# An encoder layer in split float32 on one core: merge, up and output projections rearranged, attention records stored by SyncE's queue

## What is computed

```
h = rmsnorm(x) ; z = h @ w_in
a = pool_mixer(z[:, :512]) @ w_up_pool            # 4 window sizes, 128 channels each
o_g, lse_g = dilated window attention, 3 groups of 4 heads (width 64)
b = (sum_g softmax_g(lse)_g * o_g) @ w_up_attn    # "merge": 256 channels
gates = sigmoid(h @ w_gate + b_gate)              # 2 x 1024 channels, g_a and g_b
x = x + (g_a*a + g_b*b) @ w_out
x = x + (silu(h2 @ w_ffn_gate) * (h2 @ w_ffn_up)) @ w_ffn_down,  h2 = rmsnorm(x)
y = rmsnorm(x)
```

## Time and profile before

| what | value |
|---|---|
| three runs | 2791.15, 2797.35, 2797.04 us; median 2797.04 us |
| profiled execution | 2793.5 us, span 2791.7 us |
| mean granted TensorE clock | 0.971 of 2.4 GHz |
| busy: PE, PEld, DVE, ACT, POOL (us) | 2618.3, 2126.5, 1241.7, 1082.5, 1848.3 |
| transfers | 350.25 MB, 331.01 MB of it in SP's queue, 17.09 MB in ACT's |

### The profile page before, as it was taken

How to read it: one execution, slowest core, us unless ns; L and a number is a source line. 1 busy time by engine, 2 the same in 40 slices (tenths; PEclk the granted TensorE clock), 3 DMA queues, 4 the chain that set the end, 5 groups by cost and what they waited for, 6 DMA issues and landing times.

```text
span 2791.7 us, 33643 instructions
## 1 busy us (share of the span) xinstructions
PE 2618.3 (94%) x12048; PEld 2126.5 (76%) x12048; DVE 1241.7 (44%) x1781; ACT 1082.5 (39%) x2108; POOL 1848.3 (66%) x1354
## 2 busy tenths in 40 slices
PE   5999999889799999899969999998897999998998
PEld 5887777668688888788758877776686888887886
DVE  5743556652322222344667435566433222223446
ACT  4224554333433333244542345543334233332444
POOL 6775445414688888798767654453257888886986
PEclk9999999999899999999979999999899999999999
DMA  3443445453133333363443434453522333334534
GB/s 122 121 144 99 134 140 144 136 197 101 58 101 102 99 106 114 108 201 114 150 149 110 149 99 138 140 157 134 196 83 68 111 95 103 107 93 143 192 117 140
DMA packets 334532, 350.25 MB, mean 125 GB/s; under 512 B 16800, under 2 KB 247584, under 8 KB 332576
## 3 DMA queue, kind: packets, MB, share of 16 engines
q1 hardware_dynamic: 317088, 331.01, 37.7%
q10 hardware_dynamic: 17280, 17.09, 1.8%
HBM read 248.75 MB, written 99.29 MB: 125 GB/s over the span
## 4 chain that ended last, share of the span: by engine, by line
PE 85%; DVE 5%; DMA 3%; POOL 2%; ACT 2%; issue 2%; SPq 1%; DVEq 0%; ACTq 0%
PE ps L829 27%; PE ps L831 26%; PE ps L830 26%; PE ps L894 2%; PE ps L864 2%; PE ps L849 1%; PE ps L876 1%; DMA gl<-sp_rows 1%; DMA xb<-x 1%; DVE xb L1427 1%; DMA wu_raw<-w_up_attn 1%; DVE pw L1550 1%; SPq L478 1%; DVE rec L1604 1%; DVE Y L1647 1%
## 5 line engine op out<-in xcount | busy, mean ns | idle before, releaser
L829 PE MATMUL ps<-S,t_hi 128*128 128x512 f32 x2296 | 928.5, 404 | 19.3 <-DVE v L1486 10.6
L831 PE MATMUL ps<-S,t_lo 128*128 128x512 f32 x2296 | 898.3, 391 | 0.0
L830 PE MATMUL ps<-S,t_hi 128*128 128x512 f32 x2296 | 897.4, 391 | 0.0
L829 PEld LDWEIGHTS ps<-S,t_hi 128*128 128x128 f32 x2296 | 433.2, 189 | 126.6 <-issue 38.4
L831 PEld LDWEIGHTS ps<-S,t_lo 128*128 128x128 f32 x2296 | 432.6, 188 | 92.3
L830 PEld LDWEIGHTS ps<-S,t_hi 128*128 128x128 f32 x2296 | 433.8, 189 | 78.7
L673 POOL TENSOR_TENSOR t_lo<-wraw,t_hi 128x512 fp32r<-128x512 f32 x190 | 249.0, 1311 | 265.0 <-ACT t_hi L1124 262.4
L673 POOL TENSOR_TENSOR t_lo<-wraw_ff,t_hi 128x512 fp32r<-128x512 f32 x220 | 282.8, 1286 | 77.0 <-ACT t_hi L1124 72.7
L1124 ACT CAST t_hi<-wraw_ff 128x512 fp32r<-128x512 f32 x220 | 137.0, 624 | 375.0 <-PE ps L831 372.3
L673 POOL TENSOR_TENSOR t_lo<-R,t_hi 128x512 fp32r<-128x512 f32 x154 | 232.1, 1511 | 64.5 <-ACT t_hi L1124 64.5
L1674 DVE TENSOR_TENSOR d_lo<-d_raw,d_hi 128x512 fp32r<-128x512 f32 x154 | 166.7, 1085 | 213.5 <-ACT d_hi L1294 213.5
(11 more groups left out here) (152 smaller groups left out, 4228.7 us busy)
## 6 DMA issues: line engine op xcount, KB each, us to landing
d_raw<-d_rows SPq DMA_DIRECT2D x154, 256.0 KB, 3.2
d_rows<-act_f SPq DMA_DIRECT2D x110, 256.0 KB, 2.1
wraw<-w_in SPq DMA_DIRECT2D x44, 512.0 KB, 6.1
wraw_ff<-w_ffn_gate SPq DMA_DIRECT2D x44, 512.0 KB, 4.8
wraw_ff<-w_ffn_up SPq DMA_DIRECT2D x44, 512.0 KB, 4.7
R<-w_ffn_down SPq DMA_DIRECT2D x88, 256.0 KB, 3.1
sp_rows<-gst SPq DMA_DIRECT2D x80, 256.0 KB, 2.5
wo_raw<-w_out SPq DMA_DIRECT2D x36, 512.0 KB, 3.2
```

Of the source, the lines that this page charges most:

```text
L829: nc.tensor.matmul(o_ps, w[0], r[0], start=begins, stop=False, skip_group_check=True)
L830: nc.tensor.matmul(o_ps, w[0], r[1], start=False, stop=False, skip_group_check=True)
L831: return nc.tensor.matmul(o_ps, w[1], r[0], start=False, stop=ends, skip_group_check=True)
```

## The change

**Records.** ACT only copies the unit's result; SP issues the store, in its list for product m the store of unit m - 67 (the unit is copied beside product m - 1). `load_records` stays at its place.

**Merge.** A batch takes six products in place of four; DVE does four of the six scalings, one per product, ACT the other two, as 16 activations of 64 columns each. The sums of batch 0 come at product 123, of batch 1 at 129. Transposes come after products 127 and 131. The mixer's rows 0 to 2 are loaded when batch 0 is merged, row 3 when both are, and each is split on its own.

**Up.** The first two steps' weights are loaded at product 120. The order of half steps on PE begins a0, a1, b0, b1, then as before. The first product waits for each k tile alone. SP loads up weights one step earlier in its list. On ACT a step is: `up_hi(j+2)`, the first sigmoid of j+1, `y_high(j)`, the second sigmoid of j+1. `out_hi(0)` follows at step 5, `out_hi(1)` at step 6.

**Out.** x is loaded in four parts between the tiles of `w_out`, after the last up product. Low parts 16 and 17 go from POOL to DVE, `mix_last` for pair 1 goes ahead of low part 15. The last three visits of round 3 are done for tile 6 and then for tile 7, and tile 6 is added and normed by itself.

**FFN.** The first four activation tiles of the down products are split within the last pair on ACT and DVE; the stores of the last activations move one down product later on SP.

```diff
-MT_AFTER = {MERGE0 + 9: 0, MERGE0 + 10: 1}
+MT_AFTER = {MERGE0 + 9: 0, MERGE0 + 13: 1}
+UP_ORDER = [(0, 0), (1, 0), (0, 1), (1, 1)] + [(j, a) for j in range(2, TT) for a in range(2)]
...
+N2_LAST = {(t, 21 + v): [15 + 3 * n + v] for n, t in enumerate(OUT_ROUNDS[-1][0]) for v in range(3)}
...
-        wu_at = [(XR + 20480, XR + 23552, XR + 26624), (WR + 16384, WR + 19456, WR + 22528)]
+        wu_at = [(XR + 25600, XR + 28672, XR + 20480), (WX + 12288, WX + 16640, XR + 16384)]
...
+            def store_record(s, unit):
...
+                sp.wait_ge(o_ready, due("o_ready", s, unit + 1))
...
+                sp.dma_start(by_res[qb // n, (qb % n) * P:(qb % n + 1) * P, :], o_st[:, unit % 4, :]
+                             ).then_inc(o_stored[unit % 4], 16)
...
+                    if 0 <= m - ATT0 - 2 < N_UNITS:
+                        store_record(s, m - ATT0 - 2)
...
-                    if m == MERGE0 + 9:
-                        sp.wait_ge(merged, due("merged", s, 2))
-                        for g in range(4):
-                            sp.dma_start(ml[g][:, :], mix_rows[g]).then_inc(ml_in[g], 16)
+                    if m == MERGE0 + 2:
                         load_up(s, 0)
+                        load_up(s, 1)
+                    if m == MERGE0 + 6:
+                        sp.wait_ge(mix_stored, due("mix_stored", s, 8))
+                        load_mixed(s, range(3), 1)
+                    if m == MERGE0 + 13:
+                        load_mixed(s, range(3, 4), 2)
...
-                sp.wait_ge(prod_done, due("prod_done", s, FRONT))
-                load_up(s, 1)
+                sp.wait_ge(t_ready, due("t_ready", s, FRONT))
+                load_gates(s, 1)
+                load_up(s, 2)
...
                 for j in range(2, TT):
-                    load_up(s, j)
+                    if j + 1 < TT:
+                        load_up(s, j + 1)
                     load_gates(s, j)
-                    if j == 5:
+                    if j == 4:
...
-                sp.wait_ge(up_full, due("up_full", s, 4 * (TT - 1)))
-                for t in range(TT):
-                    sp.dma_start(X[:, t, :], x_t[s, t]).then_inc(xr_in, 16)
-                for op in range(2, N_WO):
+                load_out(s, 2)
+                load_out(s, 3)
+                sp.wait_ge(up_full, due("up_full", s, 4 * TT))
+                for op in range(4, N_WO):
+                    if op < 8:
+                        for t in (2 * op - 8, 2 * op - 7):
+                            sp.dma_start(X[:, t, :], x_t[s, t]).then_inc(xr_in, 16)
                     load_out(s, op)
...
-                    if m == N_PROD + 2:
+                    if m == N_PROD + 3:
                         store_products(s, steps - 1)
...
                 mix_first(s, 1, 1)
                 out_low(s, 14)
+                mix_last(s, 1, 1)
                 out_low(s, 15)
-                mix_last(s, 1, 1)
-                out_low(s, 16)
-                out_low(s, 17)
...
+                for t in OUT_ROUNDS[-1][0]:
+                    for visit in range(len(VISITS) - 3, len(VISITS)):
+                        out_products(s, visit, (t,))
+                        part_transposes(s, 1, N2_LAST[t, visit])
...
+            def merge_scale(s, batch, pairs):
+
+                act.wait_ge(coef_ready, due("coef_ready", s, batch + 1))
+                r, g = rec[batch], GROUPS - 1
+                for q in pairs:
+                    for t in range(4):
+                        for h in range(2):
+                            o = r[:, t, 2 * g + q, h * HEAD:(h + 1) * HEAD]
+                            i = 4 * t + 2 * q + h
+                            ins = nc.scalar.activation(o, o, ACT.Copy, scale=d3[:, g, i:i + 1])
+                ins.then_inc(scaled, 1)
...
+                    if n == N_PAIRS - 1 and o > 2:
+                        part_hi(s, N_PROD + o - 3)
...
-                act.wait_ge(prod_done, due("prod_done", s, max(m - 3, N_PROD - 1)))
                 if d in (2, 3):
                     act.wait_ge(t_ready, due("t_ready", s, N_PROD))
+                elif d > 3:
+                    act.wait_ge(prod_done, due("prod_done", s, m - 3))
...
+                    if m in (MERGE0 + 2, MERGE0 + 3, MERGE0 + 8, MERGE0 + 9):
+                        merge_scale(s, (m - MERGE0) // 6, [(m - MERGE0) % 2])
+                    if m == MERGE0 + 4:
+                        up_hi(s, 0)
+                        up_hi(s, 1)
...
                 for j in range(TT):
-                    if j + 1 < TT:
-                        sigmoids(s, j + 1)
                     if j + 2 < TT:
                         up_hi(s, j + 2)
+                    if j + 1 < TT:
+                        sigmoid(s, j + 1, 0)
                     y_high(s, j)
-                    if j == TT - 2:
+                    if j + 1 < TT:
+                        sigmoid(s, j + 1, 1)
+                    if j in (TT - 3, TT - 2):
+                        out_hi(s, j - TT + 3)
```

More of the change, by code:

```diff
@@ L86, in pool_step @@
     return (e, stage) if 0 <= e < len(POOL_JOBS) else (None, None)
+UP_ORDER = [(0, 0), (1, 0), (0, 1), (1, 1)] + [(j, a) for j in range(2, TT) for a in range(2)]
+UP_COUNT = {(j, a, h): 2 * n + h + 1 for n, (j, a) in enumerate(UP_ORDER) for h in range(2)}
 OUT_ROUNDS = (((0, 1, 2), range(8)), ((3, 4, 5), range(7, -1, -1)), ((6, 7), range(8)))
@@ L254, in encoder @@
         both = [at(f"both{r}", WX + 4096 + 4096 * r, [4, 2, P]) for r in range(2)]
-        ml = [at(f"ml{g}", XR + 4096 * g, [T]) for g in range(4)]
+        ml = [at(f"ml{g}", XR + o, [T]) for g, o in enumerate((0, 4096, 8192, 12288))]
         mix_hi = [at(f"mix_hi{g}", SP_ * g, [T], F32R) for g in range(4)]
@@ L974, in pair_banks, with up_products, out_products @@
                     last[bank0(n) + b] = (reader[0], s, reader[1])
-            def up_products(s, j):
+            def up_products(s, j, a):
                 pe.wait_ge(wu_ready, due("wu_ready", s, j + 1))
                 r = j % 2
-                for c in range(4):
-                    h, b = c % 2, 4 * r + c
-                    first, rows = (0, list(zip(mix_hi, mix_lo))) if c < 2 else (4, list(zip(m_hi, m_lo)))
-                    if j == 0 and c == 0:
-                        pe.wait_ge(mixed_ready, due("mixed_ready", s, POOL_GROUPS))
-                    if j == 0 and c == 2:
-                        pe.wait_ge(mT_ready, due("mT_ready", s, 4))
+                first, rows = ((0, list(zip(mix_hi, mix_lo))), (4, list(zip(m_hi, m_lo))))[a]
+                for h in range(2):
+                    b = 4 * r + 2 * a + h
+                    if j == 0 and a == 1:
+                        pe.wait_ge(mT_ready, due("mT_ready", s, 2 * h + 2))
                     bank_read(b)
                     for k, hl in enumerate(rows):
+                        if j == 0 and a == 0 and h == 0:
+                            pe.wait_ge(mixed_ready, due("mixed_ready", s, k + 1))
                         w = [t[r][:, first + k, :] for t in (wu_hi, wu_lo)]
-                        ins = three(ps[:, b, :], w, [a[:, half(h)] for a in hl], k == 0, k == len(rows) - 1)
+                        ins = three(ps[:, b, :], w, [x[:, half(h)] for x in hl], k == 0, k == len(rows) - 1)
                     ins.then_inc(up_full, 1)
-                    last[b] = ("a_read" if c < 2 else "b_read", s, 2 * j + h + 1)
-            def out_products(s, visit):
+                    last[b] = (("a_read", "b_read")[a], s, 2 * j + h + 1)
+            def out_products(s, visit, tiles):
                 rnd, k, op = VISITS[visit]
-                tiles, v = OUT_ROUNDS[rnd][0], visit % 8
+                v = visit % 8
                 pe.wait_ge(wo_ready, due("wo_ready", s, op + 1))
@@ L1001, in out_products @@
                 r = SLOT_OF[op]
-                for idx, t in enumerate(tiles):
+                for t in tiles:
                     for n in range(2):
-                        b = 2 * idx + n
+                        b = 2 * OUT_ROUNDS[rnd][0].index(t) + n
                         if v == 0:
@@ L1392, in _ @@
                     ff_pair(s, n)
-                for m in range(N_PROD, N_PROD + 4):
-                    part_hi(s, m)
                 for m in range(N_PROD, N_OPS):
@@ L1648, in gated, with add_projected @@
                                  Y[:, :, 3:7:2, c].bitcast(F32), ALU.subtract).then_inc(y_ready, 1)
-            def add_projected(s, rnd):
-                for idx, t in enumerate(OUT_ROUNDS[rnd][0]):
+            def add_projected(s, *tiles):
+                for t in tiles:
                     for n in range(2):
@@ L1723, in _ @@
                         pooled_low(s, e)
[L1724 to L1739 removed]
+                    batch, step = divmod(m - MERGE0, 6)
+                    if batch in (0, 1):
+                        if step == 0:
+                            merge_differences(s, batch)
+                        elif step == 1:
+                            merge_coefficients(s, batch)
```

(16 more changed lines are left out.)

137 lines of the change are left out of this document (68 added, 69 removed).

## The result

The changed kernel takes **2715.96 us** (median of 4 runs, 2712.18 to 2717.12) against 2795.66 us for the kernel before on the same chip: ratio 0.9715, 95% interval 0.9698 to 0.9732. The forecast was 2712, its range 2686 to 2752. Where a difference is small I read the waits in the trace, not the time.

The account below looks back on a forecast made before the run. PE was taken to bound the kernel, busy 2618.3 of 2791.7 us. Gains of 26 + 30 + 18 + 9 = 83 us gave 2710.5 from the profiled execution or 2714 from the median; forecast 2712 us, range 2686 to 2752.

Parts of the forecast that it names:

- A, merge: Merge to first up product: waits for product 124's addition and the first up product go; gain 26 us, bounds 11 to 32.
- B, up: Up and first out round: gates' cycle shortens from 10.9 to 8.3 us a step; gain 30 us, bounds 14 to 39.
- The walk: Up steps followed at 8.3 us each from the first up product, giving new waits of 4.6 us a sequence.
- Rival 1: Up: the gates' cycle stays the bound at 9.1 us a step; 20 us less gain, 2732 us; chance 20%.
- C, last out round: Last out round: waits behind POOL's low parts and part of the last norm's go; gain 18 us, bounds 5 to 25.
- D, first down products: First down products: old waits go, about 4 us comes at the sixth; gain 9 us, bounds 5 to 14.
- Records: Record stores moved to SP's queue: landings of at most 6.9 us within 8.1 of cover; cost 0, up to 10.
- rival 5: Records in SP's queue land too late and slow the products with units; 2816 us at 10.3 us landing; chance 5%.
- rival 2: Merge keeps a wait, ACT standing in line for up weights and coefficients; 19 us less gain, about 2731; chance 13%.
- rival 3: All four stretches run dry of waits, upper bounds summing to 110 us; 2684 us; chance 7%.
- rival 4: Waits only change names, no part giving more than 2 us; 2790 us; chance 4%.
- Clock: PE time at the lower 1.2 GHz level, tied to waits, comes back: 2.6, 7, 3.5 and 1.5 us by window.

Follow-up runs that it names:

- edit 10: Changed kernel with the second batch's record loads three products later, behind the stores of two results: 2709.7 us, ratio 0.9699.
- edit 3: Changed kernel with both sigmoids of step j+1 ahead of the rounding of Y of step j on ACT: 2725.87 us, ratio 0.9752.
- the repeat: The changed kernel measured once more, with nothing altered: 2718.92 us, ratio 0.9730.
- edit 8: Changed kernel with all eight loads of x in one block ahead of the fifth `w_out` tile: 2731.39 us, ratio 0.9770.
- edit 6: Changed kernel with low parts 16 and 17 back on POOL, behind part 15: 2726.41 us, ratio 0.9754.
- edit 5: Changed kernel with the last three out visits done for tiles 6 and 7 together on PE: 2719.25 us, ratio 0.9726.
- edit 9: Changed kernel with the stores of the last activations' sums two down products later on SP: 2712.19 us, ratio 0.9708.
- Edit 1: Changed kernel with records stored from ACT's queue again, at once after the copy: 2717.95 us, ratio 0.9723.
- edit 2: Changed kernel with ACT's share of the merge scalings back on DVE, in the new order: 2719.16 us, ratio 0.9728.

## Why the prediction was right

**A, merge** (26; 25.2). The mechanism is right. The wait on product 124's addition is 0.2 us and the first up product waits for nothing. The late start stayed as said, with 1.75 and 0.54 us behind it, and edit 10 shows its cause. But the sum comes out so near by luck in part: 2.5 of the 25.2 us lie ahead of the merge, where the forecast had nothing. The merge gave 22.6: 1.83 and 1.85 us on ACT's copy of `u` in the second batch were not in the sum (ACT copies when DVE has written `gst`, which now stands between scalings), and its clock gave 3.4 us where 5.2 were booked. The fourth mixer row was ready in sequence 1 but 1.88 us late in sequence 2, which falls in B. That the early mixer rows and weights took out the 5.37 us before the first up product rests on the trace; no edit undoes them.

**B, up** (30; 27.2). The walk named waits of 0.6, then 1.0 and 1.0 to 2.6, and up to 1 for x; these add up to 2.6 to 5.2, and the 4.6 it used is not worked out further. The trace has 1.07, then 0.52 (on DVE's `gl`, which the walk did not have), 0.94 and 1.26: 3.8. The mechanism is right and the term that was mis-sized is the clock: 7 us were taken in each sequence, and it gave 6.6 in sequence 1 and 5.4 in sequence 2, where seven matmuls behind the 1.88 us wait for the mixer row run at the lower level. What the lower bound was built on was wrong too: a cycle of 9.1 us was to cost 16, and edit 3 shows a cycle of 9.3 that costs 7 (10 against the first median). Rival 1 would have been a smaller loss than its 2732. The price of moving x, "up to 1 us" at the later visits, held, but only for loads in turns with `w_out`: in one block they cost 12.5 us against the repeat (edit 8), so it is not the bytes but their order that decides.

**C, last out round** (18; 19.0). The list of what is left was 1.0 + 0.5 + 1.5 + 5.7; it is 0.97 + 0.76 + 1.01 + 6.22, besides 1.3 of small ones that were there before. Edit 6 puts the low parts on DVE at 7.5 us of it or more, so of C's parts this is the large one; `mix_last` took 2.3 us of waits in each sequence. The tile split was to take 1.5 us off the wait for the norm and to cost 1.5 for part 17; by edit 5 it takes 1.4 and costs 1.0.

**D, first down products** (9; 5.0, its lower bound). Both old waits went, and one of 3.58 and 3.40 us stands at the sixth product, where I took 4, for the reason given (edit 9). Missed were 1.07 us at the third, twice, for two sums of activations that POOL makes ahead of its low part. The clock was mis-sized as well: I booked a gain of 1 us, and D lost 0.7, since the down stage has 1.2 us more busy time than before (423.9 us before, 425.1 after, both sequences).

**Records** (0; 0). Edit 1. The reading behind it was wrong and did no harm: 6.9 us was taken for the longest landing of a record's store and is that of a load; the longest store took 6.0.

**The rivals.** Rival 1's pace did not come: a step takes 8.2 to 8.5 us and only the one with the two loads of `w_out` 9.05 and 9.75. Nor did rival 5's landings. Waits from the merge to the first up step did stay, as rival 2 had it, 7.85 us of them, but not by its mechanism: edit 10 leaves ACT's list as it is and they fall to 1.5, so it was DVE's late start that made them and not ACT standing in line for weights. Nor did all waits go (rival 3) or only change names (rival 4).

**Clock.** 5.2 + 14 + 7 + 1 = 27.2 us were booked; 4.9 + 11.9 + 7.3 - 0.7 = 23.5 came, to the rounding. In the second window of the earlier trace rows a clock of 0.94 went to 1.00 when the four waits of 2.4 to 4.2 us went. Behind the wait of 3.58 us that ended at 1152.30 the first matmul takes 0.59 us to the start of the next and the six after it 0.43 each, the lower level. But the length of a wait does not settle it: behind 1.07 us at 1140.25 the matmuls keep 0.23 us, and behind 3.40 us in sequence 2 no run of slower ones shows, while shortly behind 1.85 us at 1861.82 seven matmuls in a row take 0.43.

## What to carry to other kernels

Where one engine is busy for most of the span (94% here), list its waits with the step that is ahead of each in *another* engine's order, and move that step: nearly all of the 76 us came from order and from moving a few operations to another engine (edit 6), none from less work on PE. The clock that came back with the waits is 23.5 of them. In a queue that works in order, what stands ahead of a small transfer sets its time, so put bulk loads in groups with the small ones between (edits 8 and 10), and put stores that wait for something behind the loads that don't (edit 9). A producer's cycle that is slower than the engine it feeds seems to cost its lag over all steps less the lead it starts with (edit 3 alone speaks for it), so count both before pricing it.

## What the runs showed of the hardware that I had not expected

**Small DVE operations take on POOL's length.** POOL and DVE in the kernel after, between two products of the merge:

```profile
507.93 1.30 POOL L705 TENSOR_TENSOR t_lo<-wraw,t_hi 128x512 fp32r<-128x512 f32 x1 [0.90 <-ACT t_hi L1162]
...
507.95 1.30 DVE L1642 TENSOR_TENSOR den<-wden 128x16 f32<-128x16 f32 x1
509.29 0.17 DVE L1643 TENSOR_TENSOR den<-den,wden 128x16 f32<-128x16 f32 x1
```

Two operations on 16 columns, one after the other: the one that begins 0.02 us behind a POOL operation of 1.30 us takes 1.30, the next, in the gap before POOL's next at 509.31, takes 0.17. The trace here agrees with the Trainium skill (SBUF — State Buffer, Who interferes with whom), by which the engine that starts second waits for the other's whole operation. The loss here is set by the length of the other engine's instruction, so small operations lose most for their size.

**ACT's small scalings are no bargain by the element.** Eight of 64 columns take 2.02 us, 0.25 each; one scaling of DVE's covers the same 512 columns in 0.69 us (at 513.89 in the kernel after) to 1.81 (at 510.72). By edit 2 they bring nothing that the time shows.

**A store behind loads in one queue.** The store issued at 482.93, behind eight record loads, held its buffer until DVE went on at 490.53; with half the loads ahead of it (edit 10) it was issued at 480.01 and DVE did not wait. The store at 482.93, from issue to landing, in the kernel after:

```profile
DMA to landing us min/median/max: 7.5/7.5/7.5
```

The store at 473.88, ahead of the record loads, took 2.3 us, and the one at 480.01 in edit 10 took 5.0. So of the 5.4 us by which edit 10 lands its store sooner, 2.9 are time in SP's list and 2.5 are time in the queue. The Trainium skill (DMA: Bandwidth & Descriptors, Queues, rings and completion order) has one queue's ring worked through in order; the traces agree, the store landing at 490.4, behind the last record load at 488.9.
